# Dividing the lower part of every weight panel by columns between VectorE and GpSimd

## The reference, cut to what matters

```python
z = h @ even_w_in[j] + even_b_in[j]                       # layer 0: gating and a 31 tap convolution
x = x + jnp.concatenate([ya, yb], axis=-1) @ even_w_out[j]
u = causal_dwconv(h @ w_up, conv_w, conv_b)               # conv_ffn, in both layers: 3 taps, D_FF = 2816
gate, val = jnp.split(u, 2, axis=-1)
x = x + (jax.nn.silu(gate) * val) @ w_down
qkv = (h @ odd_w_qkv[j]).reshape(bn, s, 3, ATTN_HEADS, HEAD_DIM)   # layer 1: dilated attention
x = x + o @ odd_w_o[j]
```

## Time and profile before

| | |
|---|---|
| median of 3 runs | 1527.44 us (1526.49 to 1530.45) |
| the profiled execution | 1524.76 us |
| its span, first to last instruction | 1522.6 us |
| granted TensorE clock, mean | 0.992 |
| PE busy | 1445.0 us (95%) |
| DVE busy | 765.3 us (50%) |
| ACT busy | 572.7 us (38%) |
| POOL busy | 286.1 us (19%) |

### The profile page before, as it was taken

The page is one execution under the profiler, slowest core; times in us unless marked ns, Lnnn a source line. Parts: engine busy times, 40 slices in busy tenths (PEclk is TensorE's granted clock), DMA queues, the critical chain, the costliest instruction groups (busy, mean ns, idle before and its releaser), DMA issues.

```text
span 1522.6 us, 28468 instructions
## 1 busy us (share of the span) xinstructions
PE 1445.0 (95%) x11258; PEld 1208.2 (79%) x11258; DVE 765.3 (50%) x1406; ACT 572.7 (38%) x930; POOL 286.1 (19%) x118
## 2 busy tenths in 40 slices
PE   7988999999989999999999999998999999989896
PEld 5867999999948999998999888998566566555554
DVE  4954888648574888635463546644122222212122
ACT  3255555445354555437663126344111111111111
POOL 0001222212201122225863003772000000000000
PEclk9999999999999999999999999999999999999998
DMA  8684545664443555643543213668999999999995
GB/s 315 238 306 164 166 165 166 196 246 153 153 180 97 186 185 175 212 154 111 181 139 98 84 42 111 207 208 338 427 425 422 427 423 425 427 426 425 424 426 219
DMA packets 72097, 375.82 MB, mean 247 GB/s; under 512 B 8128, under 2 KB 8384, under 8 KB 49984
## 3 DMA queue, kind: packets, MB, share of 16 engines
q1 hardware_dynamic: 72000, 374.43, 65.3%
HBM read 373.35 MB, written 1.05 MB: 246 GB/s over the span
## 4 chain that ended last, share of the span: by engine, by line
PE 61%; issue 19%; SPq 7%; DMA 6%; DVE 5%; ACT 1%; POOL 1%; POOLq 0%; DVEq 0%; ACTq 0%
PE lin L692 9%; PE lin L693 8%; PE lin L694 8%; PE stat L1431 4%; PE mixp L1404 4%; PE mixp L1408 4%; DMA moe_low<-in_experts 4%; SPq L609 4%; PE lin L711 2%; PE stat L1364 2%; PE lin L1374 1%; DMA moe_high<-in_experts 1%; PE stat L692 1%; PE mixp L692 1%; PE mixp L693 1%
## 5 line engine op out<-in xcount | busy, mean ns | idle before, releaser
L692 PE MATMUL lin<-r_hi,w_hi 128*128 128x256 f32 x1464 | 425.4, 291 | 10.5 <-POOL w_lo L1875 5.1
L693 PE MATMUL lin<-r_lo,w_hi 128*128 128x256 f32 x1464 | 415.5, 284 | 0.0
L694 PE MATMUL lin<-r_hi,w_lo 128*128 128x256 f32 x1464 | 415.4, 284 | 0.0
L692 PEld LDWEIGHTS lin<-r_hi,w_hi 128*128 128x128 f32 x1464 | 282.0, 193 | 20.3 <-POOL w_lo L1875 6.7
L693 PEld LDWEIGHTS lin<-r_lo,w_hi 128*128 128x128 f32 x1464 | 282.3, 193 | 0.8
L694 PEld LDWEIGHTS lin<-r_hi,w_lo 128*128 128x128 f32 x1464 | 282.1, 193 | 0.0
L1875 POOL TENSOR_TENSOR w_lo<-ring,w_hi 128x1024 fp32r<-128x1024 f32 x43 | 110.7, 2575 | 560.4 <-ACT w_hi L1478 297.3
L1879 POOL TENSOR_TENSOR w_lo<-ring,w_hi 128x1024 fp32r<-128x1024 f32 x71 | 175.1, 2484 | 191.0 <-ACT w_hi L1472 190.9
L1908 DVE TENSOR_TENSOR w_lo<-ring,w_hi 128x1024 fp32r<-128x1024 f32 x129 | 161.6, 1257 | 85.8 <-ACT w_hi L1478 65.5
L1478 ACT ACTIVATE w_hi<-ring 128x1024 fp32r<-128x1024 f32 x124 | 129.7, 1049 | 57.3 <-PE mixp L694 49.1
L1472 ACT ACTIVATE w_hi<-ring 128x1024 fp32r<-128x1024 f32 x119 | 124.1, 1050 | 34.2 <-PE lin L694 16.7
(11 more groups left out here) (477 smaller groups left out, 2719.6 us busy)
## 6 DMA issues: line engine op xcount, KB each, us to landing
ring<-in_panels SPq DMA_DIRECT2D x272, 512.0 KB, 4.0
moe_low<-in_experts SPq DMA_DIRECT2D x64, 1024.0 KB, 22.8
moe_high<-in_experts SPq DMA_DIRECT2D x22, 2048.0 KB, 24.8
aring<-in_ada SPq DMA_DIRECT2D x24, 1024.0 KB, 6.0
ring<-in_experts SPq DMA_DIRECT2D x20, 1024.0 KB, 26.9
moe_high<-in_experts SPq DMA_DIRECT2D x20, 1024.0 KB, 22.0
cst<-in_experts SPq DMA_DIRECT2D x10, 1280.0 KB, 24.0
sq<-in_experts SPq DMA_DIRECT2D x10, 1024.0 KB, 29.5
```

The costliest lines, as they stand in the source:

```text
L692: pe.matmul(o, w_hi[:, slot, c], r[0], start=start, stop=False, skip_group_check=True)
L693: pe.matmul(o, w_hi[:, slot, c], r[1], start=False, stop=False, skip_group_check=True)
L694: return pe.matmul(o, w_lo[:, slot, c], r[0], start=False, stop=stop, skip_group_check=True)
```

## The change

Every subtraction before the second block is made in two parts: VectorE takes columns 0 to 767 and GpSimd columns 768 to 1023. Panels from 188 on stay with GpSimd alone. TensorE and SyncE now wait for both semaphores of such a panel. VectorE's calls for panels in slot 3, which returned at once, now make an instruction; GpSimd's loop of 43 subtractions of 1024 columns becomes a loop with four subtractions of 256 columns in a round, 172 in all.

```diff
-POOL_SLOT = 3
-def on_pool(n):
-    return n % RING == POOL_SLOT or n >= CHAIN2
-def lower_parts(n, pool):
-    return sum(is_split(m) and on_pool(m) == pool for m in range(n))
+DVE_PART = 768
...
         def wait_split(eng, n, it=None):
-            event = w_split_pool if on_pool(n) else w_split
-            v = lower_parts(n, on_pool(n)) + 1
-            eng.wait_ge(event, v if it is None else it * (1 if on_pool(n) else RING - 1) + v)
+            v = splits_before(n) + 1
+            eng.wait_ge(w_split_pool, v if it is None else it * RING + v)
+            if n < CHAIN2:
+                eng.wait_ge(w_split, v if it is None else it * RING + v)
...
         def _(pool):
-            first = OUT0 + (POOL_SLOT - OUT0) % RING
-            with pool.Fori(0, (CHAIN2 - first + RING - 1) // RING) as it:
-                pool.wait_ge(w_hi_ready, it * RING + (splits_before(first) + 1))
-                pool.tensor_tensor(w_lo[:, POOL_SLOT, :], ring[:, POOL_SLOT, :], w_hi[:, POOL_SLOT, :].bitcast(F32),
+            def lower_part(n, it=None):
+                v = splits_before(n) + 1
+                part = slice(DVE_PART, D)
+                pool.wait_ge(w_hi_ready, v if it is None else it * RING + v)
+                pool.tensor_tensor(w_lo[:, n % RING, part], ring[:, n % RING, part], w_hi[:, n % RING, part].bitcast(F32),
                                    ALU.subtract).then_inc(w_split_pool, 1)
+            rounds = (CHAIN2 - OUT0) // RING
+            with pool.Fori(0, rounds) as it:
+                for j in range(RING):
+                    lower_part(OUT0 + j, it)
+            for n in range(OUT0 + rounds * RING, CHAIN2):
+                lower_part(n)
...
             def split_lo_loop(n, it=None):
-                if on_pool(n):
+                if n >= CHAIN2:
                     return
                 v = splits_before(n) + 1
+                part = slice(0, DVE_PART)
                 dve.wait_ge(w_hi_ready, v if it is None else it * RING + v)
-                dve.tensor_tensor(w_lo[:, n % RING, :], ring[:, n % RING, :], w_hi[:, n % RING, :].bitcast(F32), ALU.subtract)\
-                    .then_inc(w_split, 1)
+                dve.tensor_tensor(w_lo[:, n % RING, part], ring[:, n % RING, part], w_hi[:, n % RING, part].bitcast(F32),
+                                  ALU.subtract).then_inc(w_split, 1)
```

## The result

The changed kernel takes 1517.85 us on the median of 15 runs (1511.49 to 1526.3), the kernel before 1527.42 on the median of 15 beside them: a ratio of 0.9934, with 0.9922 to 0.9945 as its 95% interval. That is 9.6 us less, where 9.1 were forecast (1518.3 us). The profiled execution took 1515.16 us around a span of 1513.4.

A forecast was written before the change was run, and what follows sets the result against it. Layer 0 was taken as bound by VectorE's serial round with one hold of 1.97 us. Gaps -9.2, attention +0.33 and output product -0.27 sum to -9.1: 1518.3 us from 1527.44, eight in ten between 1516.0 and 1524.0.

The forecast's parts named there:

- term of -9.2 for 77 matmuls: Layer 0's up product: TensorE's gaps, 77 matmuls of 0.12 us lost against layer 1, should go: -9.2 us.
- VectorE's round in layer 0: Layer 0's up product: VectorE's 12.58 us round becomes 10.87 plus 0.8 of new holds, 11.67, against TensorE's 11.52.
- first rival: Layer 0's gaps go only in part, some appear in layer 1: holds near 1.25 a round, -3.5 us, 1524 us; chance 0.12.
- GpSimd's part alone: GpSimd's subtraction of 256 columns, undisturbed: 0.72 us, of which 0.57 excludes VectorE.
- The signs: Right: equal matmul windows, no early `w_lo` waits, `hid_hi` 0.3 to 0.5 us. Wrong: GpSimd parts over 1 us, holds every round.
- Layer 1's up product: Feed-forward of layer 1: no gap before, so no gain; VectorE's round is 10.87 by the same sum; cost 0.
- lead of 3.2 us: Up products: an excess of VectorE's round over TensorE's costs nothing until it has added up to 3.2 us.
- Attention: Attention's chain: three VectorE subtractions of 0.87 us replace two of 1.14, +0.33 us.
- Output product: Layer 0's output product: TensorE's wait for VectorE's subtraction gets 0.27 us shorter.
- Convolution: Panels 16 and 17: two holds of 0.57 us delay its end by at most 1.14, hidden behind TensorE; taken as 0.
- ScalarE's lateness: No-change rival: ScalarE's late silu and `w_hi` set layer 0's gaps, which stay: 0 to +0.4 us, 1527.6; chance 0.07.
- The slower rival: Both up products: each of four GpSimd parts holds VectorE 0.57 us, round 13.15, +17 us, 1544 us; chance 0.10.

The follow-up runs named there:

- e3: Kernel before, whole panels by turns, but GpSimd's subtraction of a slot 3 panel made as four instructions of 256 columns: 1519.49 us, ratio 0.995.
- e5: Changed kernel plus a GpSimd subtraction of 768 constant columns, read by nobody, in each of 16 rounds over panels 24 to 87: 1522.92 us, ratio 0.9965.
- e4: Changed kernel, but VectorE alone makes every subtraction up to panel 187 and GpSimd none of them: 1517.91 us, ratio to before 0.9932.
- e1: Changed kernel, but divided 768 to 256 only up to panel 89, whole panels by turns from 90 to 187: 1514.78 us, ratio to before 0.9916.
- e6: Changed kernel, but in the attention's panels 114 to 117 VectorE takes 32 columns and GpSimd 992: 1514.89 us, ratio to before 0.9921.
- e9: Changed kernel, but divided only up to panel 89, turns from 90 to 187, panels 114 to 117 whole on GpSimd: 1515.49 us, ratio 0.9935.

## Why the prediction was right, point by point

**The bound and the cause: shown.** Layer 0's gaps were the loss, and they came from VectorE's serial round with one hold of 1.97 us in it. e3 cuts the hold from 1.97 to 0.31 us without moving any work, e5 puts one back without moving any, e4 takes away GpSimd; the three agree. The term of -9.2 for 77 matmuls measured -9.37.

**VectorE's round in layer 0: the sum right, its terms not.** 11.67 was forecast, 11.73 measured. But the holds are 1.29 in place of 0.8, and the round without them 11.73 - 1.29 = 10.44 in place of 10.87; e4's round, with no holds at all, was also put 0.34 too high (11.95, against 11.61 in layer 1). Which term of that sum is too large no run shows apart. The two errors nearly cancel, and that was luck: holds of 1.29 meet the condition of my own first rival (near 1.25 a round, a round of 12.12, -3.5 us in all). Its loss did not come only because the rest of the round was shorter than I had summed. GpSimd's part alone was right (0.72 forecast, 0.74 measured). Which operations meet a hold I had foreseen only in part. Where VectorE waits for `w_hi`, GpSimd does queue behind it, as forecast: VectorE starts at 182.07, GpSimd at 182.12, and GpSimd's two parts take 2.40 us where they take 2 x 0.74 alone. But in the other half of the round GpSimd starts its part 0.3 us before VectorE comes to its own, and holds subtraction and copy in turn, two full holds of 0.55.

The rule of the Trainium skill that I had weighed (SBUF — State Buffer, Who interferes with whom), that the later engine stands until the first has finished its instruction, is what these rows show: 0.55 at 256 columns, 1.1 at 512. The warning of the Trainium skill's page Perfetto Trace Analysis (Optimizing Scalar/DVE Operations) that work moved between the two may not help came true at 512 columns, where it cost, and at 256 it would have been misleading: both parts of a panel run one after the other there too (from 175.68 to 177.50, 1.82 us, against 1.22 undivided), and the kernel was still faster. e4 bears the warning out in another way: without any GpSimd work the time is the same.

**The signs.** The window, the waits of TensorE, GpSimd's part and the three subtractions came out as written. `hid_hi` did not: 0.3 to 0.5 us on the mean was the sign of being right, and it is 0.63 (the group in 130 to 290 us):
```profile
L1969 DVE CAST hid_hi<-sgf 128x256 f32 x22 | 13.9, 630 | 0.0
```
Two of the signs of being wrong appeared as well, `hid_hi` and `w_lo` held in every round, and gaps in layer 1. Neither decided: the holds left no gap in layer 0, since the rest of the round was shorter than I had summed, and the gaps of layer 1 are 1.5 us.

**Layer 1's up product: the step that failed in size.** I put it at 0, since the same lead of 3.2 us was to absorb 0.15 a round. It cost 1.5: 0.34 where the product begins and 1.18 later. The round is 11.82 us there, 0.3 over TensorE's 11.52 and not 0.15. Ten such rounds are 3.0, which a lead of 3.2 would still have covered; but the first gap comes at panel 155, after eight rounds, so the lead was 8 x 0.3 = 2.4 us, and each later round loses 0.3. The beginning I had not costed at all: there is no lead yet, and TensorE waits for a panel's second part, which runs behind the first. The timeline of PE where panel 124 begins:
```profile
485.06 0.28 PE L685 MATMUL lin<-r_hi,w_lo 128*128 128x256 f32 x1
485.57 0.39 PE L683 MATMUL lin<-r_hi,w_hi 128*128 128x256 f32 x1 [0.23 <-POOL w_lo L1869]
```
The matmuls stand 0.51 apart in place of 0.12. e1, which has turns in this layer, has neither cost.

**Attention: right.** Forecast +0.33; measured +1.07, of which 0.74 is put down to the clock stretch at 413.9 us. Two traces bear that out: e5 has the same code there without a stretch and takes 0.35 more than before, and e1, with before's code and a stretch, takes 0.73 more. The timeline of DVE has the three subtractions of 0.87 from step to step:
```profile
417.10 1.82 DVE L1910 TENSOR_TENSOR w_lo<-ring,w_hi 128x768 fp32r<-128x768 f32 x2
...
421.10 0.96 DVE L1910 TENSOR_TENSOR w_lo<-ring,w_hi 128x768 fp32r<-128x768 f32 x1
```
e4, with three of 1.14, gives +1.15 by the same sum (1.14 expected). The sum holds for links made longer or more; for links taken away it does not, as e6 and e9 show: 2.28 was promised and 1.0 to 1.1 came.

**Output product: right,** -0.23 against -0.27. **Convolution: right, at 0.** GpSimd's two parts at 77.86 did hold VectorE: the last twelve operations took 6.28 us after and 5.58 before. But the mean starts at 80.58 after and 80.48 before, behind TensorE's own work.

**The sum.** The work's own difference is -7.75 in the two traces where -9.1 was forecast: the 1.5 of layer 1 explain it. The medians nevertheless differ by 9.6. In the profiled pair the remaining -1.6 are +0.7 of clock stretches and -2.25 of the pause at the end. Whether the change moves these on the average is not settled. The mean granted clock differs little: 0.9899 over the 15 runs of the changed kernel, 0.9902 over 34 runs of before. The interval of the ratio is 1.8 us to either side, about as much as lies between 9.6 and 7.75. So the closeness of 1518.3 to 1517.85 is partly luck.

**The rivals.** The gaps didn't stay in part in layer 0, and not in full; ScalarE's lateness was a consequence. The slower rival did not come about with 256 columns, because only two of four holds are full: 1.29 a round, below the 1.43 from which it decides, and 1.43 was worked out with a round 0.43 too long. With 512 its mechanism did: 3.5 a round, and 15.6 us slower (0.0102 x 1527.2). That this is near its +17 is chance, since the +17 was summed for holds of 2.28 on a longer round.

## What to carry to other kernels

When two engines exclude each other, look at the longest instruction on the engine with time to spare, not at its load: cut it into pieces that fit between the other's operations, or drop it, before you balance work. Divide a step over such engines only if the sum of holds in a round stays under the slack of the serial engine's round; count a full hold for each piece that starts just ahead of the other's. And where a product begins, with no panels in store, count the parts of a panel one behind the other.

## What the runs showed of the hardware

- One hold costs VectorE nearly what GpSimd's instruction has left: 1.97 us of 2.10 behind 1024 columns, 1.27 of 1.41 in e5, 0.55 of 0.68 behind 256; up to 1.1 behind 512. GpSimd is held in the same way where it starts second (2.40 us for two parts at 182.12).
- A GpSimd subtraction of float32 in SBUF takes 0.47 us for 128 columns, 0.74 for 256 and 2.42 for 1024, so about 0.2 and 2.2 ns a column.
- In this kernel I had not expected VectorE alone to be as fast as both engines: 0.9932 (0.992 to 0.9945) against 0.9934 (0.9922 to 0.9945).
- Stretches at a granted clock of 0.5, 3.4 to 6.8 us each apart from the last one, stand at partly different places in the traces. Here they moved single stages by 0.5 to 1.6 us, so a difference between two traces in one stage is not yet a cost of the change: the other traces decide.
